# One slot fewer in the weight ring of an expert-choice encoder block, and affT at the other end of the memory

## The reference

```python
cap = EC_FACTOR * n_tok // N_EXPERTS            # 32 tokens of the prompt, 128 of the sample
aff = jax.nn.softmax((xf @ w_router).astype(jnp.float32), axis=-1)
gate, idx = lax.top_k(aff.T, cap)
xs = xf[idx]
hdn = jax.nn.silu(jnp.einsum('ecd,edf->ecf', xs, w_gate)) * jnp.einsum('ecd,edf->ecf', xs, w_up)
out = jnp.einsum('ecf,efd->ecd', hdn, w_down) * gate[..., None].astype(x.dtype)
y = jnp.zeros_like(xf).at[idx.reshape(-1)].add(out.reshape(-1, D))
```

## Time and profile before

| | |
|---|---|
| time, median of 3 runs | 2841.53 us (2840.67 to 2841.87) |
| the profiled execution | 2841.87 us, span of its instructions 2840.1 us |
| mean granted clock of TensorE | 0.978 |
| busy, share of the span | TensorE 95%, DVE 65%, ACT 49%, POOL 18% |
| moved by DMA | 686.26 MB, mean 242 GB/s |
| expert stage | from about 1334 us to the end |

### The profile page before, as it was taken

How to read it: one execution, slowest core, us unless ns; L and a number is a source line. 1 busy time by engine, 2 the same in 40 slices (tenths; PEclk the granted TensorE clock), 3 DMA queues, 4 the chain that set the end, 5 groups by cost and what they waited for, 6 DMA issues and landing times.

```text
span 2840.1 us, 44592 instructions
## 1 busy us (share of the span) xinstructions
PE 2689.6 (95%) x18224; PEld 2151.9 (76%) x18224; DVE 1849.7 (65%) x2309; ACT 1395.4 (49%) x1769; POOL 519.4 (18%) x492
## 2 busy tenths in 40 slices
PE   7999999988999979993999999999999999999997
PEld 5788887877877858882777777777777777777775
DVE  7212232768888756557676776776676676677787
ACT  2212221865554343332565565566565566567674
POOL 2001030004453433331000000000000000011233
PEclk9999999999999989996999999999999999999998
DMA  6478875766565554335688788888788788889992
GB/s 230 167 201 232 255 250 142 165 228 234 179 221 185 176 203 134 126 108 231 230 305 288 273 304 299 277 287 304 275 308 286 271 307 306 283 292 332 334 332 102
DMA packets 237452, 686.26 MB, mean 242 GB/s; under 512 B 18729, under 2 KB 65208, under 8 KB 232128
## 3 DMA queue, kind: packets, MB, share of 16 engines
q1 hardware_dynamic: 219904, 627.96, 63.1%
q0 software_dynamic: 17344, 55.44, 7.4%
HBM read 577.46 MB, written 105.88 MB: 241 GB/s over the span
## 4 chain that ended last, share of the span: by engine, by line
PE 48%; DMA 2%; POOL 1%; DVE 1%; issue 1%; ACT 0%; POOLq 0%; ACTq 0%; DVEq 0%
PE moe_strip L2449 12%; PE moe_up L2464 4%; PE moe_gate L2466 4%; PE moe_up L2465 4%; PE moe_gate L2464 4%; PE moe_gate L2465 4%; PE moe_up L2466 4%; PE moe_down L2464 4%; PE moe_down L2466 4%; PE moe_down L2465 4%; PE moe_turn L2424 1%; DMA out<-moe_norm_x 1%; DVE pieces_low L2658 1%; PE moe_turn L2387 0%; DMA y<-moe_out_p,moe_at_out 0%
## 5 line engine op out<-in xcount | busy, mean ns | idle before, releaser
L2658 DVE TENSOR_TENSOR pieces_low<-pieces_raw,moe_high 128x1024 fp32r<-128x1024 f32 x768 | 903.0, 1221 | 382.5 <-PE moe_strip L2449 246.6
L2550 ACT ACTIVATE moe_high<-pieces_raw 128x1024 fp32r<-128x1024 f32 x768 | 769.0, 1052 | 310.9 <-PE moe_up L2466 196.2
L2449 PE MATMUL moe_strip<-pieces_raw,moe_xT_p 128*32 128x256 f32 x4096 | 232.7, 382 | 0.5 <-ACT moe_xT_p L2562 0.5
L2464 PE MATMUL moe_down<-moe_high,moe_hdn 128*128 128x512 f32 x512 | 208.4, 407 | 0.1
L2464 PE MATMUL moe_gate<-moe_high,moe_xT 128*128 128x512 f32 x512 | 203.6, 398 | 1.4 <-DVE pieces_low L2658 1.4
L2449 PEld LDWEIGHTS moe_strip<-pieces_raw,moe_xT_p 128*32 128x32 f32 x4096 | 136.8, 110 | 89.3 <-issue 10.5
L2464 PE MATMUL moe_up<-moe_high,moe_xT 128*128 128x512 f32 x512 | 204.4, 399 | 0.0
L2466 PE MATMUL moe_down<-pieces_low,moe_hdn 128*128 128x512 f32 x512 | 200.7, 392 | 0.0
L2465 PE MATMUL moe_down<-moe_high,moe_hdn 128*128 128x512 f32 x512 | 200.4, 391 | 0.0
L1031 POOL TENSOR_TENSOR hg_W<-hg_E 128x640 f32<-128x640 f32 (+1 forms) x92 | 163.8, 1807 | 198.5 <-PE hg_l L1098 101.4
L2466 PE MATMUL moe_gate<-pieces_low,moe_xT 128*128 128x512 f32 x512 | 200.0, 391 | 0.0
(11 more groups left out here) (349 smaller groups left out, 5710.4 us busy)
## 6 DMA issues: line engine op xcount, KB each, us to landing
pieces_raw<-in_w_gate_e SPq DMA_DIRECT2D x128, 1024.0 KB, 5.2
pieces_raw<-in_w_up_e SPq DMA_DIRECT2D x128, 1024.0 KB, 5.9
pieces_raw<-in_w_down_e SPq DMA_DIRECT2D x128, 1024.0 KB, 5.4
bias_fx<-xs SPq DMA_DIRECT2D x40, 1024.0 KB, 5.4
fr_raw<-in_w_in SPq DMA_DIRECT2D x16, 1024.0 KB, 8.8
ws<-fr_late_split SPq DMA_DIRECT2D x32, 512.0 KB, 4.6
bias_fw<-ws SPq DMA_DIRECT2D x32, 512.0 KB, 8.2
mo_gates<-h SPq DMA_DIRECT2D x20, 512.0 KB, 4.4
```

Of the source, the lines that this page charges most:

```text
L2449: last = nc.tensor.matmul(strip_ps[j * CP:(j + 1) * CP, kind, :], x, raw[g % RAW][:, k * D + j * STRIP:k * D + (j + 1) * STRIP], start=sta ...
L2464: nc.tensor.matmul(to[:], x_k[:, kk, 0:CS], hi, start=(kk == 0), stop=False)
L2550: nc.scalar.activation(high[:, g % HI, cols], raw[g % RAW][:, cols], ACT.Copy).then_inc(hi_done, 1)
L2658: nc.vector.tensor_tensor(low[g % RAW][:, cols], raw[g % RAW][:, cols], high[:, g % HI, cols].bitcast(F32), ALU.subtract).then_inc(lo_done, 1)
```

## The change

The ring has 12 slots in place of 13, so `load_first_pieces` loads 12 pieces in `stage_choose`, the loader of the expert stage begins with piece 12, and each load waits for `sample_mm >= g - 11`, not `g - 12`. `affT` is no longer placed at the right with `best` and `at`, before the recurrence, but at the left among the tensors that live to the end of the kernel, after the recurrence; what is placed left after it, the ring too, starts 2 KB per partition higher. Nothing else is edited.

```diff
--- before.py
+++ after.py
@@ -2025,7 +2025,7 @@
                 dve.wait_ge(picked, EARLY_PICKS)
 
 
-RAW, HI = 13, 4
+RAW, HI = 12, 4
 QUADS, HALVES = 4, 2
 COLS = D // HALVES
 STRIP = D // QUADS
@@ -2830,8 +2830,8 @@
 
             stage_attention(nc, ident, h, qk, table, aT, pair, pair_in, load_filler)
             pairs.close()
-            best, at, affT = (routing.enter_context(nc.sbuf_tensor(f"route_{n}", [AFF_ROWS, cols], dt, side="right"))
-                              for n, cols, dt in (("best", TOK, F32), ("at", TOK, U32), ("affT", AFF_COLS, F32)))
+            best, at = (routing.enter_context(nc.sbuf_tensor(f"route_{n}", [AFF_ROWS, TOK], dt, side="right"))
+                        for n, dt in (("best", F32), ("at", U32)))
             wroom = mix.enter_context(nc.sbuf_tensor("wroom", [P, SLOTS * D], F32, side="right"))
             w_in_room = [nc.alloc_semaphore(f"mo_w_ready{n}") for n in range(SLOTS)]
 
@@ -2846,6 +2846,7 @@
         gates = [s.sb(f"gates{n}", [CAPS[n], NE]) for n in range(2)]
         picks = [s.sb(f"picks{n}", [CAPS[n], NE + 1], U32) for n in range(2)]
         gates4, picks4 = s.sb("gates4", [P, NE]), s.sb("picks4", [P, NE], U32)
+        affT = s.sb("affT", [AFF_ROWS, AFF_COLS])
         stage_mix_out(nc, ident, h, aT, o, norm_g, w_na, w_hg, w_out, xln, ln1_g, ln1_b, w_router, x1, y, affT, best, at,
                       wroom[:].rearrange("p (n d) -> p n d", d=D), w_in_room)
         mix.close()
```

## The result

The changed kernel takes 2854.61 us (median of 6 runs, 2851.72 to 2861.91) against 2841.70 us for before in the same comparison (6 runs, 2840.04 to 2844.22). The ratio is 1.0055, 95% interval 1.0045 to 1.0065: slower, by 12.9 us between the medians. The profiled execution of the changed kernel took 2851.21 us with a span of 2849.4 us, 9.3 us over the span of before. It is shorter than each of the six, so its trace shows less than the median loses. A further 16 executions of the changed kernel on record, without runs of before beside them, took 2854.05 to 2862.02 us.

The account below looks back on a forecast made before the run. The prediction took TensorE's own work to bound the expert loop. Middle sessions 10.8 plus last session 1.0 less start 1.2 gave 10.6 us on 2841.87, 2852.5, or 2852.1 for the median; range 2844 to 2863 us.

Parts of the forecast that it names:

- The bound: Expert loop: TensorE's own work end to end, busy 1436.7 of 1439 us; any added stall comes out in full.
- The loads move by one step and nothing else does: Ring loads: same issue moments, each for piece g-1 instead of g, so each piece's load starts 2.7 us later.
- Which sessions: Middle sessions of experts 1 to 14: eighth piece late by 0.77 us on average, 10.8 us in all.
- Why the loads take 9 us there: Before the middle session: the previous expert's accumulating scatters occupy the DMA engines, so loads take 9 us, median 5.2.
- The last session: Last session of the kernel: its last load starts a step later, costing 1 us, between 0 and 2.
- The start: Start of the loop: one load fewer before the first gather gains 1.2 us, between 0 and 3.
- The clock in the loop: Expert loop: clock stays at 1.00; rival, falls in each of 14 sessions add 24 us, 2876 us, chance 0.03.
- The size: Whole kernel: 10.6 us slower, 2852.1 us or +0.37%; chance of being slower 0.85.

Follow-up runs that it names:

- the ring alone: The kernel before with 12 ring slots and affT left where it was: 2860.25 us, ratio 1.0045 to before.
- the step alone: The kernel before, 13 slots and memory unchanged, with the loader waiting one piece longer for each load: 2857.32 us, ratio 1.0039 to before.
- scatters held back: The changed kernel with POOL's scatters of experts 0 to 11 waiting for the next expert's middle session: 2848.62 us, ratio 1.0007 to before.
- both cures: The changed kernel with scatters of experts 0 to 11 delayed and loads 9 to 11 issued behind the first gathers: 2842.97 us, ratio 1.0008 to before.

## Why the prediction was right

*The bound.* TensorE's loop had nothing to give away, and each stall came out at the end. Right: 11.8 us of longer middle sessions stand against a span that grew by 9.3.

*The loads move by one step and nothing else does.* Right, and it is shown by the run with 13 slots and a later wait. In expert 7 the load of the eighth piece of the changed kernel is issued at 2014.0, 2.6 us before its session, and lands 8.8 later; in the earlier trace rows the load of the next piece is issued 2.6 us before the session and takes 9.0. The lateness per session was forecast at 0.4 to 1.5 us with a mean of 0.77; the trace has 0.12 to 1.65 and 0.91 over 13 sessions. That the means lie so close is in part luck, as two small errors work against each other. The prediction had the eighth piece read 5.89 us after the session's start, by cutting the session in eight equal parts; in the session of expert 14 of the changed kernel, which has no stall, its matmuls start 6.07 us after it. With 6.07 the eleven landings of the first trace give a mean of 0.55, and 14 x 0.55 = 7.8 us. The landings themselves then came 0.15 us later than the shift by one step says (0.70 us for the same eleven sessions), and another 0.08 us a session go between the landing and the session's end.

*Which sessions.* Nearly right: 14 were named, 13 lost time in this trace, two of them without a row in the waits view. Expert 14, the one with the norm tiles' traffic, was in time by 0.26 us here, and lost 0.3 to 1.7 us in four of five other traces with one step less (the ring alone, the step alone, scatters held back, the changed kernel again; nothing with both cures).

*Why the loads take 9 us there.* The scatters were argued from the earlier trace rows and are shown by the run that moves them: 5.4 us instead of 9.0 for the load ahead of the eighth piece's, 5.0 instead of 9.5 for the one behind it.

*The last session.* This term was mis-sized: 1 us forecast, with 2 as its bound. Its rows, with the load of the last piece by line:

```profile
2784.87 6.25 PE L2449 MATMUL moe_strip<-pieces_raw,moe_hdn_p 128*32 128x256 f32 x112
2794.07 1.07 PE L2449 MATMUL moe_strip<-pieces_raw,moe_hdn_p 128*32 128x256 f32 x16 [2.95 <-DMA pieces_raw<-in_w_down_e]
```

```profile
L2053 SPq DMA_DIRECT2D pieces_raw<-in_w_down_e x1: 367/367/367, 2781.8 to 2781.8; - x1
DMA to landing us min/median/max: 12.2/12.2/12.2
```

The load takes 12.2 us, where 9 to 11 were taken for the range, and the session lasts 10.27 us instead of 7.11: it loses 3.16. Part comes back: the idle time of 3.35 us at 2801.4 in the earlier trace rows, where TensorE waited for DVE, isn't there any more. TensorE arrives later at a result that was late anyway. A wait of 1.95 us for `moe_hdn` stands near 2827 instead, and at the end 1.6 us are left.

*The start.* 1.2 us forecast, 1.2 us earlier at the second session, but not by the sum's own way. The wait fell by more, from 12.2 to 10.6 us, and with 0.4 us that stood before the first load the first session starts 2.0 us earlier (1345.8, not 1347.8). But more of it runs at the low clock, and it lasts 10.0 us instead of 9.1. In both traces the clock rises near 1352; these are the windows of the changed kernel on either side, the clock last but two. So part of the earlier start was time at half speed. That the two numbers agree is luck. The prediction's picture of 13 MB still draining when the gather is issued was too large as well: the tenth load had landed at 1335.4, so that at most three were in front of the gather of 1336.4. In the first trace the gather was through when TensorE began at 1344.4, before the thirteenth load landed at 1345.1, so it didn't stand behind all of them. Yet they cost it time: one load less took 1.1 to 1.6 us off the wait, two less 3.8.

```profile
1347.00:1351.00 4.00, 4.00 (x44) 0.50 0.57 165
1352.00:1356.00 4.00, 3.79 (x72) 1.00 0.00 0
```

*The clock in the loop.* The loop's stalls of up to 1.45 us of idle time left it at 1.00, as the row at 853.3 said. The one of 2.95 us in the last session was followed by a fall (0.51 from 2795.5 for 3.4 us), which fell into the tail.

*The size.* 10.6 us forecast, 12.9 measured between the medians, and 11 to 14 us in the three other comparisons of kernels with the same step. By terms, the first trace has 11.8 us for the middle sessions (10.8 forecast), 1.6 for the last session and its tail (1.0), -1.2 for the start (-1.2), and -2.9 that nobody had forecast (see below); without the last the sum would be 12.2. Why the six runs lie as far apart as 2851.7 to 2861.9 us isn't shown. In the four traces of kernels with one step less and nothing else the middle sessions lose 11.7 to 13.4 us in sum, though a single one can differ by over 2 us between them (expert 13 loses 0.7 with the step alone and 3.5 with the ring alone); so the stalls alone, as traced, don't explain 10 us; and before spreads too, over 4 us in its first 6 runs and over 10.7 in the 33 of a later comparison. One source has nothing to do with the ring: the first load of a piece is issued anywhere from 1305.9 to 1310.6 us in the twelve traces.

*Left open.* The stretch from an expert's first session to its middle one was 29.5 us in the first trace of before, 29.3 in both of the changed kernel, and 29.6 in those of the ring alone, the step alone, the ring of 11 and the scatters held back; it was 29.3 again in the last runs. The difference lies inside the expert's first session, which lasts 7.11 us where the stretch is 29.3 and 7.3 to 7.45 where it is longer, with no wait in the profile. It follows neither the ring nor the place of `affT`, and it is worth 3 to 4 us. It may go with the chip: the four traces with 29.6 come from one chip, on which the median of before was also 4.6 to 5.4 us above its medians on the two other chips of the experiments, and the six traces from those two have 29.3. But no kernel was traced on both kinds, and of the two first traces the chips aren't on record. What makes it isn't known. In the sum of these two it flatters the changed kernel by 2.9 us.

## What to carry to other kernels

Ask of a ring not how many buffers it has but when the youngest buffer of the next reader is issued, counted in pieces of work ahead of that reader, and compare this with the slowest landing at that place, not the median: here the 3.3 us that a load of median length keeps with the smaller ring were enough only where no load took 9 us, and one session in three had one. As long as the issue moves but the traffic doesn't, the trace of before prices it: the next buffer's landing, held against this buffer's use. Where the margin is short because of another queue's transfers, moving those is the cheaper cure: with the ring of 13 the late scatters cost nothing that could be told (0.9990 beside 0.9988), and a deeper ring costs memory.

## What the runs showed of the hardware

Two accumulating scatters, 128 rows of 4 KB and 128 of 1 KB, lengthen the landing of 1 MB loads issued around them from 5.0 to some 9 us. In expert 7 of the changed kernel four loads in a row take 9.4, 9.0, 8.8 and 9.5 us, until the loads pause; the one behind the pause takes 4.8. That the delay lasts so long because the loads ask for 388 GB/s of some 426 is an argument from the earlier trace rows, not tried by itself.

In front of these strip matmuls the idle time of TensorE in the waits view is 0.21 us shorter than what the session loses (1.45 of 1.66, 2.95 of 3.16). The step from a load's landing to the first matmul that waited for it was 0.04 us, in the middle sessions of all the experts.

How long TensorE sat idle doesn't tell by itself whether the clock falls. It stayed at 1.00 behind 1.45 us in the changed kernel, behind 2.2 us in expert 13 with the scatters held back, and behind 2.71 us in the last session with the ring alone. It fell behind 2.4 us in expert 13 of that same trace, behind 2.95 us in the last session of the changed kernel, and behind 1.92 us, a wait for DVE ahead of expert 15's first session, in the changed kernel run again. With a ring of 11 it fell in expert 3 behind two idle times of 1.4 us with 16 matmuls between them, and stayed at 1.00 in expert 6 behind 2.24 and 1.44 us. These are the windows behind the 2.71 us (ring alone) and behind expert 6 (ring of 11), the clock last but two:

```profile
2801.00:2804.40 3.40, 3.37 (x26) 1.00 0.15 43
1953.20:1956.60 3.40, 3.40 (x27) 1.00 0.00 0
```
